# Seven value tiles of a paged cache: a quarter of their pieces moved from the SP and ACT queues to the Pool queue

## What is computed

```
past = cache_nsa_kv[page_table].reshape(B, past_len, 4, G, dk)
full = jnp.concatenate([past, kv[:, :, :4].astype(past.dtype)], axis=1)
p_s = masked_softmax(s_s, mask_s)
o_s = jnp.einsum('bqghnr,bqgnrd->bqghd', p_s.astype(v_sel.dtype), v_sel)
```

## Time and profile before

| | before |
|---|---|
| runs | 2198.90, 2199.69, 2202.35 us |
| median | 2199.69 us |
| the profiled execution: its own time | 2196.9 us |
| its span, first to last instruction | 2195.2 us |
| busy: PE / DVE / ACT / POOL | 94% / 28% / 18% / 14% |
| mean granted TensorE clock, as a share of full speed | 0.962 |
| HBM read / written | 195.38 MB / 18.42 MB |

### The profile page before, as it was taken

One profiled execution on the slowest core, in us unless ns is written; L12 is line 12 of the kernel. 1 busy time (PEld: TensorE's weight loads), 2 busy tenths in 40 slices (PEclk: granted clock), 3 DMA queues, 4 the chain that ended last, 5 costly groups with the idle time before them and its releaser, 6 DMA issues.

```text
span 2195.2 us, 28391 instructions
## 1 busy us (share of the span) xinstructions
PE 2054.6 (94%) x11212; PEld 1713.2 (78%) x11212; DVE 611.8 (28%) x1084; ACT 403.9 (18%) x839; POOL 315.7 (14%) x523
## 2 busy tenths in 40 slices
PE   6999998899999999999889999899739999999997
PEld 5888887788888888888766668686417888888886
DVE  3455456211121000010237753344401221110002
ACT  2344443210000000100225433233200100000000
POOL 2233324000000000000036653340000000000000
PEclk9999999899999999999959999999969999999999
DMA  5222232012222222214350009986891122222221
GB/s 135 74 73 61 69 98 70 19 68 77 76 76 76 77 76 76 76 39 175 96 138 2 1 11 228 184 186 207 269 319 58 39 77 76 67 58 70 74 76 39
DMA packets 216473, 206.83 MB, mean 94 GB/s; under 512 B 13857, under 2 KB 170642, under 8 KB 216242
## 3 DMA queue, kind: packets, MB, share of 16 engines
q1 hardware_dynamic: 197938, 188.67, 30.8%
q10 hardware_dynamic: 18432, 16.79, 2.3%
HBM read 195.38 MB, written 18.42 MB: 97 GB/s over the span
## 4 chain that ended last, share of the span: by engine, by line
PE 85%; DVE 3%; ACTq 3%; SPq 2%; issue 2%; DMA 2%; ACT 1%; POOL 1%; DVEq 0%; POOLq 0%
PE ps L828 51%; PE ps L867 10%; PE ps L1046 5%; PE ps L1039 2%; PE ps L907 2%; ACTq L1671 2%; PE ps L817 2%; PE ps L1100 1%; PE ps L882 1%; PE ps L1122 1%; PE ps L1140 1%; ACTq L342 1%; DMA stream<-in_cache_nsa_kv 1%; PE ps L1248 1%; PE ps L933 1%
## 5 line engine op out<-in xcount | busy, mean ns | idle before, releaser
L828 PE MATMUL ps<-h,stream 128*128 128x260 f32 x2688 | 592.7, 384 | 1.7 <-DVE h L2260 1.7
L828 PEld LDWEIGHTS ps<-h,stream 128*128 128x128 f32 x2688 | 512.3, 191 | 81.5 <-DVE h L2260 2.1
L828 PE MATMUL ps<-big,stream 128*128 128x260 f32 (+1 forms) x2464 | 542.9, 383 | 4.6 <-DVE big L1937 3.9
L828 PEld LDWEIGHTS ps<-big,stream 128*128 128x128 f32 (+1 forms) x2464 | 466.8, 190 | 80.4 <-issue 5.1
L867 PE MATMUL ps<-h,stream 128*128 128x260 f32 x1024 | 236.8, 386 | 5.1 <-DVE h L1792 5.1
L867 PEld LDWEIGHTS ps<-h,stream 128*128 128x128 f32 x1024 | 191.6, 192 | 37.2 <-issue 10.0
L1411 ACT ACTIVATE scratch<-x 128x520 f32<-128x520 f32 x32 | 20.4, 637 | 1052.6 <-DVE x L1925 1052.6
L1925 DVE TENSOR_TENSOR x<-x,ps 128x520 f32 x32 | 22.3, 696 | 537.7 <-PE ps L828 522.1
L1934 DVE SCALAR_TENSOR_TENSOR scratch<-ps,rstd 128x520 f32<-128x520 f32 x64 | 44.8, 700 | 343.2 <-PE ps L828 343.2
L1046 PE MATMUL ps<-big 128*128 128x256 f32 x384 | 99.7, 383 | 0.0
L2106 DVE COPY big<-ps 128x512 f32<-128x512 f32 x80 | 55.3, 691 | 101.1 <-PE ps L1039 78.3
(11 more groups left out here) (308 smaller groups left out, 2032.7 us busy)
## 6 DMA issues: line engine op xcount, KB each, us to landing
stream<-in_w_mlp_up SPq DMA_DIRECT2D x16, 2048.0 KB, 8.3
stream<-in_w_mlp_down SPq DMA_DIRECT2D x16, 2048.0 KB, 8.9
stream<-in_cache_nsa_kv SPq DMA_DIRECT2D x128, 256.0 KB, 6.1
stream<-in_w_hgrn_in SPq DMA_DIRECT2D x32, 512.0 KB, 6.9
stream<-in_cache_nsa_kv SPq DMA_DIRECT2D x128, 128.0 KB
stream<-in_cache_nsa_kv ACTq DMA_DIRECT2D x128, 128.0 KB
stream<-in_cache_win_kv SPq DMA_DIRECT2D x16, 512.0 KB
out<-in_cache_win_kv SPq DMA_DIRECT2D x8, 1022.0 KB
```

Source lines behind the costliest of these rows:

```text
L828: m = nc.tensor.matmul(pair(c)[0:n1, a, :], w[:, k, P * c_local:P * c_local + n1], rhs[:, k, NH * a:NH * a + NH], start=(k == 0), stop=(k ...
```

## The change

For tiles 13 to 19, the fourth page (`c` = 3) of each of the four samples, 4 pieces of 16, is issued by Pool after the end of its program. SP and ACT each issue 6 pieces of these tiles where they issued 8. Pool's pieces raise semaphores of their own, `pool_in`, one for each slot, and PE waits for both counts before it multiplies a tile. Tile 12 stays as it was.

```diff
+        pool_in = [sem(f"pool_in{s}") for s in range(4)]
...
-            return 16 * sum(WINDOW_DMAS if n in (0, 1, 10, 11) else PAGE_DMAS for n in range(i % 4, i + 1, 4))
+            return 16 * sum(WINDOW_DMAS if n in (0, 1, 10, 11) else PAGE_DMAS - (4 if n >= 13 else 0) for n in range(i % 4, i + 1, 4))
+
+        def pool_count(i):
+
+            return 16 * 4 * len([n for n in range(i % 4, i + 1, 4) if n >= 13])
...
-            def load_rows(i, js):
+            def load_rows(i, js, count=4):
...
-                    for c, page in enumerate(page_numbers(mybir.EngineType.SP, first_page(i, j), 4)):
+                    for c, page in enumerate(page_numbers(mybir.EngineType.SP, first_page(i, j), count)):
...
-                load_rows(i, range(2))
+                load_rows(i, range(2), 4 if i == 12 else 3)
...
+            pool.wait_ge(pages_in, 16)
+            for i in range(13, 20):
+                slot_free(pool, i)
+                for j in range(4):
+                    page, = page_numbers(mybir.EngineType.Pool, first_page(i, j) + 3, 1)
+                    nc.gpsimd.dma_start(kv_tile(i)[:, j, 3, :], page_rows(i, j, page)).then_inc(pool_in[kv_slot(i)], 16)
...
                     pe.wait_ge(kv_in[kv_slot(i)], kv_count(i))
+                    if i >= 13:
+                        pe.wait_ge(pool_in[kv_slot(i)], pool_count(i))
...
-                    for c in range(4):
+                    for c in range(3):
                         load_page(i, j, c)
```

## The result

The changed kernel took 2181.54, 2181.95 and 2183.41 us, a median of 2181.95 against 2199.69: ratio 0.9925, 95% interval 0.9912 to 0.9939, a gain of 13 to 19 us. Measured again in the first experiment it is 0.9929 (0.9911 to 0.9948). I had forecast 2190.3 us, at the lowest 2184.5: the direction was right, the size was not. (The second measurement's median, 2184.53 us, lies at the very edge of the range; its gain is 14.2 us, where 9.4 were forecast.)

What follows compares the result with a forecast made beforehand. PE's waits for cache pieces were taken as bound by ACT's queue up to tile 17, then the 16 DMA engines. The engines' 9.4 us, less than the queue's 13.7, came off 2199.7: 2190.3 us, range 2184.5 to 2200.4.

Steps and rivals of the forecast that it cites:

- SP and ACT issue less: In tiles 13 to 19 ACT issues 42 pieces in place of 56, 12.0 us less; SP is not the later queue.
- ACT starts earlier: Two pieces fewer on SP bring tile 11's rows, and so ACT's first issue, 1.7 us earlier, at about 1586.1.
- The engines carry the same bytes: From 1587 on, 16.66 MB remain for the DMA engines at 343 GB/s: 48.6 us, a gain of 9.4 us.
- The queue's forecast alone: By ACT's queue alone, its last piece is out at 1622.1 rather than 1635.8: 13.7 us.
- Pool's price: A piece issued by Pool costs 1.7 us, and stays hidden up to 2.2 us a piece.
- Rival B: Pool is the slowest queue, deciding from 2.55 us a piece; at 3.1 us a piece, 2215.0 us, slower; chance 0.13.
- Rival A: Engines give no more than now: at 304 GB/s a gain of 3.2 us, at 284 a 0.7 us loss; chance 0.17.
- Rival C: Only the queue counts, if slabs do not disturb the last tiles: 13.7 us gain, 2186.0 us; chance 0.10.
- Costed at nothing: PE's second wait for each of seven tiles and Pool's 28 loads and waits add no time.

Runs made afterwards that it cites:

- the first experiment: The changed kernel run once more, unaltered, against the kernel before: 2184.53 us beside 2198.76, ratio 0.9929.

## Why the prediction was right in part and wrong in size

- *SP and ACT issue less: right.* 12.0 us forecast, 13.0 measured (48.02 to 35.01 us). ACT's last piece was forecast for 1622.1 and went out at 1622.39. ACT's pieces came a little faster in this profile, 0.834 us against 0.857; in the other runs with 42 issues in which ACT did not wait for slots it is 0.835 to 0.859, so the extra 1.0 us is not shown to come from the change.
- *ACT starts earlier: right.* 1.7 us forecast, and 1.7 us is what two pieces less cost SP in every profile (2.87 + 5.75 us before, 2.56 + 4.35 after). ACT's start came 2.8 us earlier in this profile (19.0 to 16.2 us behind the last key turn), as on the average of all; the other 1.1 us vary with the profile and are not shown to come from the change.
- *The engines carry the same bytes, "the term that counts": wrong, the step that failed.* ACT's start and ACT's issuing came 2.8 + 13.0 = 15.8 us earlier, and the section lost 15.9; in the second profile of the change it is 1.96 + 12.36 = 14.3, and 14.0. The queue's forecast alone was 13.7. I had held the queue's 13.7 us down to 9.4 by 16.66 MB that would have to pass, at 343 GB/s, before tile 19. What did pass from 1587 to 1632 was 31 x 311 + 14 x 365 = 14.75 MB, in 45 us at a mean of 328 GB/s. The rate was no higher than I took; the bytes were fewer, and with the slabs held back 12.1 MB were enough. At 343 GB/s, 14.75 MB are 43.0 us, a gain of 15.0, and would have left the queue's 13.7 to decide. I had charged both slabs in full to the time before tile 19, since both had landed before it in the old profile. But they are only beside the pieces, not ahead of them: with the tiles earlier, the slabs, 13.9 us behind their issue, land when the last tile begins and 6 us after, and the engines go on at 389 GB/s behind 1632. And Pool had a larger start, with the rest that was under way in that stretch: 17 x (271 - 173) = 1.67 MB by 1587, where I had counted 1.05.
- *Pool's price: too dear, without effect.* 0.91 us where I took 1.7, with the bound for hiding at 2.2. Rival B did not come about; its formula held to 3 us when Pool was slowed.
- *Rival A* fell by its time, at most 3.2 us of gain where 13 to 19 came, and not by its rate: 311 GB/s from 1587 to 1618 is near its 304. It shared the wrong bytes: 14.75 MB at 304 GB/s are 48.5 us, not 54.8. The Trainium skill's rule that spreading over queues only saves issue time (DMA: Bandwidth & Descriptors, Rules for kernel authors) agrees with the runs: issue time was what the stretch lacked, and SP could take pieces from ACT with a gain as well (7.4 us).
- *Rival C,* with a chance of 0.10, was the case that came, at its price of 13.7 us and somewhat more, but not for its reason: the slabs disturb the last pieces as before, 9.54 us behind ACT's last issue against 9.06. I tied the queue's gain to a condition that it did not need: a delay that is there before and after does not count.
- *Costed at nothing:* PE's second waits and Pool's loads cost nothing that shows, and the granted clock stayed low, 0.60 in the last tiles against 0.56.

## What to carry to other kernels

Where several queues feed one consumer, add up each queue's issues by its own pace and its own start: the one that ends last sets the time, and pieces may go from it to any queue that is ahead. A bound by bytes may count only what must have landed before the consumer can go on; transfers for later work that merely run beside it delay it by their share, and whether that delay changes is a question of its own. And once the pieces are early, move the large loads behind them, but no further than they are needed: one tile later took another 5 to 7 us off the changed kernel (2177.26 us, the lowest median here, with intervals that overlap a little), and holding both back behind tile 19 nothing, since PE then waited for the weights.

## What was not expected of the hardware

A DMA issued by Pool with a page number from a register took 0.54 us of issue and 0.91 us in all, and its 128 KB landed 4.6 us later in the median; I had expected it to cost nearly twice that. Its pieces also moved in larger packets: from 1590 to 1610 Pool's queue took 482 packets for 1.31 MB, 2.7 KB each, and SP's 2088 for 1.90 MB, 0.9 KB each.

And the mixture matters for the engines: with slabs in rows of 2 KB beside pieces in rows of 1 KB they moved 365 GB/s in the changed kernel and with slabs alone 389, with pieces alone 341 at about the same share (slabs behind tile 19), yet the pieces in the mixture came later. The packets of each queue show how the engines were shared. In the kernel before, from 1630 to 1638, SP's queue (q1) carries slabs and ACT's (q10) the last pieces; in the changed one, from 1632 to 1640, only slabs are left (packets, MB, share of the 16 engines):

```profile
q1 hardware_dynamic: 1048, 2.11, 71.8%
q10 hardware_dynamic: 1025, 0.93, 34.7%
```

```profile
q1 hardware_dynamic: 1527, 3.09, 105.1%
```

Side by side the two queues got about the same number of packets, and since a slab's packets are 2 KB and a piece's 1 KB, the slabs took two thirds of the bytes: 2.11 MB against 0.93. (The last line also shows that the share can pass 1 with one queue alone.)
